# Four pool products in front of the second part of a projection, or two in front and two inside it

## The chip, the cores and the metric

The kernel runs on one core of a Trainium2 chip. The metric is the time of one execution on the device in microseconds; before the change the median of three runs is 1624.82 us (1624.4 to 1625.36). The profiled execution took 1629.18 us, of which the trace spans 1627.4 us. The engines are TensorE (PE in the rows, PEld for its weight loads), VectorE (DVE), ScalarE (ACT), GpSimd (POOL) and SyncE (SP), which issues the weight loads from memory.

## What is computed

Two transformer blocks on 256 rows of width 2048. The change lies in the second block, in what stands between its input projection and its feed-forward part:

```python
h = rms_norm(x, g_mix)
z_pool, z_q, z_kv, z_kr, z_mq = split(h @ w_in)
y_pool = pool_mixer(z_pool, w_pool, pool_scale)   # 4 groups of 128 columns
y_mla = mla_mixer(z_q, z_kv, z_kr, ...)           # 8 heads of 128
y_mem = memory_cross_attention(z_mq, mem, ...)    # 4 heads of 128
x = x + concatenate([y_pool, y_mla, y_mem]) @ w_o
x = x + conv_glu_ffn(rms_norm(x, g_ffn), ...)

# pool_mixer, for group gi with window w:
d = (csum - lagged csum) / count - p              # difference to a running mean
y = einsum('bsgc,gcd->bsgd', d, w_pool) * pool_scale
```

So the row of 2048 values that `w_o` multiplies has sixteen pieces of 128: pieces 0 to 3 are the pool groups, 4 to 11 the heads of the latent attention ("mla"), 12 to 15 the heads of the cross attention.

## The kernel before

All data are kept transposed, 128 features on the partitions and 256 rows along the free axis. A projection is done in blocks: one block is a piece kt of the contraction (128 values) for one tile j of 128 output columns. Operands are split into a high and a low part of reduced width, and a block of the projections spoken of here is three matmuls of 256 columns, L1130 (high weights, high data), L1131 (high, low) and L1132 (low, high). Eight blocks make a "half": the weights of a half lie in a slot of `wh` and `wl`, and ScalarE makes the high part of them (L1480) and VectorE the low part (L1877) of each half, four slots in turn. SyncE loads the raw weights two halves at a time.

The order of all work is made by a planner at build time. It walks through the products, counts estimated costs of each engine, and puts the small steps of the attention heads (six lanes of tasks) between the blocks. What comes out is one list of beats, and every engine runs through its own beats of that list in that order. Nothing on an engine can pass an instruction that waits. The calls of `pool_end` stand outside the planner's costs: they put a beat into the list and take a PSUM bank, no more.

The second output projection (`w_o`) is done in three parts, since the pieces get ready at different times: "oa" contracts over kt 12 to 15, "ob" over kt 4, 5, 6, 7, 0, 1 in this order, "o2" over kt 8 to 11, 2 and 3. Each part goes over all sixteen tiles j, and each tile is then added to `xs` by VectorE (L2311). A tile takes the next of four PSUM banks in rotation (`gemm_bank`), and its first matmul waits until what stood in that bank has been taken out (`bank_clear`).

A pool group ends in `pool_end`: TensorE multiplies the group's 128 x 256 values with its 128 x 128 matrix in full width (L1451, recorded as two passes), VectorE scales the result out of PSUM (L2323), ScalarE writes its high part (L1837), VectorE its low part (L2325). In VectorE's program the scale waits for the product and the low part for ScalarE, before the next group's scale is come to:

```python
e.wait_ge(*after(t, "pe", "mm"))
e.tensor_scalar(y, ps[bank][:, 0:T], v_("pool_scale", g), None, ALU.mult)
e.wait_ge(*after(t, "act", "hi"))
e.tensor_tensor(hB2[:, g, T:2 * T], y, hB2[:, g, 0:T].bitcast(F32), ALU.subtract)
```

Around the change the list reads: the last tiles of "oa"; the value tile "uv" of heads 4 to 7 in banks 3 and 0, which ScalarE copies out (L1755); steps of heads 4, 6 and 7 (scores of head 6, norm of head 4); `pool_end` of groups 0 to 3 in banks 1, 2, 3, 0; weight split 227; "ob" 0 in bank 1, with the maximum of head 6; "ob" 1 to 3 in banks 2, 3, 0, and between their blocks the splits 228 and 229, the scores of head 4 (L1345) after fifteen blocks of "ob", head 4's maximum (L2078 on VectorE), the rest of head 7's norm; after "ob" 3 the turning of head 6's probabilities (L1352), split 230, the first block of "ob" 4, the scores of head 7, the copy of head 6's turned probabilities out of PSUM (L1623 on ScalarE), the next block, and head 6's product of probabilities and values (L1356, L1358). Heads 4 to 7 are pieces 8 to 11, so they have to be ready for "o2". Behind "o2" stands the sum of squares for the next norm: ScalarE squares each tile (L1827), GpSimd adds them up (L2434), and TensorE sums over the partitions (L1393).

Of the kernel before, what the change touches and what calls it, by code (L numbers as in the profile page):

```python
# [17 lines left out]
KT = D // P  # L18
# [178 lines left out]
class Order:  # L197
# [219 lines left out]
    def s_tile(self, tile, buf, order=range(KT), bank=None):  # L417
        if bank is None:
            bank = self.gemm_bank()
            self.take(tile, bank)  # L420
        order = list(order)
        blocks = [(tile, bank, kt, i == 0, i == KT - 1) for i, kt in enumerate(order)]
        self.s_half(blocks[:8], buf)
        self.s_half(blocks[8:], buf)
# [67 lines left out]
def order():  # L492
    o = Order()
# [192 lines left out]
    def up(g, keys):  # L686
        hs = range(4 * g, 4 * g + 4)
        if "un" in keys:
            o.many([("un", h) for h in hs], 0, 2, "L")
        if "uv" in keys:  # L690
            banks = o.gemm_bank(), o.gemm_bank()
            for b in banks:
                o.take(("uv", g), b)
            o.m_half(("uv", g), banks, (0, 1), "L", True, True)
        if "uq" in keys:
            o.many([("uq", h) for h in hs[:2]], 8, 4, "L")
            o.many([("uq", h) for h in hs[2:]], 8, 4, "L")
        if "ur" in keys:
            o.many([("ur", j) for j in (2 * g, 2 * g + 1)], 8, 4, "L")
        o.up_half = o.half  # L700
# [5 lines left out]
    def o2_part(i, first, end):  # L706
        name, kts = O2_PARTS[i]
        blocks = []
        for j in range(first, end):
            b = o.gemm_bank()  # L710
            o.take((name, j), b)
            blocks += [((name, j), b, kt, kt == kts[0], kt == kts[-1]) for kt in kts]
        for u in range(0, len(blocks), 8):
            o.s_half(blocks[u:u + 8], "D")
# [12 lines left out]
    def pool_end(g, bank):  # L727
        o.take(("pf", g), bank)
        o.beat("pf", g, bank)
# [25 lines left out]
    o.until(*[("mem", j) for j in range(4)])  # L755
    o2_part(0, 0, KT)
    up(1, ("uv",))
    for g in range(4):
        pool_end(g, o.gemm_bank())
    o.until(*[("mla", h) for h in range(4)])  # L760
    o2_part(1, 0, KT)
    o.until(*[("mla", h) for h in range(4, 8)])
    o2_part(2, 0, KT)
    o.o2_half = o.half
# [50 lines left out]

def program(nc, table, wts, ada, xN, xT, memN, crow, cst, vec, msk, wpool, dt, out):
    o = order()
    with ExitStack() as ctx:
        at = [nc.sbuf_base + (-nc.sbuf_base) % 32]
# [1769 lines left out]
```

## Time and profile before

| what | value |
|---|---|
| median of three runs | 1624.82 us (1624.4 to 1625.36) |
| the profiled execution | 1629.18 us |
| its span in the trace | 1627.4 us |
| TensorE busy | 1581.8 us (97%) |
| VectorE busy | 1154.2 us (71%) |
| ScalarE busy | 861.7 us (53%) |
| GpSimd busy | 139.6 us (9%) |
| DMA, mean over the span | 203 GB/s |

Shares are of the span. Busy time of TensorE is modelled from pipelined matmuls, so the stretches and the starts of instructions say more of its pace than its busy share. The granted clock is given as a share of full speed; 0.50 is 1.2 GHz and 1.00 is 2.4 GHz. "Idle before" in brackets is the time in which the engine stood still ahead of an instruction, with what released it. Times in the views are counted from the start of the span.

### The profile page before, as it was taken

What the parts mean: (1) busy time and instruction counts of PE and PEld (TensorE: products, weight loads), DVE (VectorE), ACT (ScalarE), POOL (GpSimd) and SP (SyncE); (2) the same over time, 40 slices, a digit from 0 to 9 for tenths busy, and PEclk for the clock granted to TensorE, in tenths of its full rate; (3) what the DMA queues carried; (4) which work ended last, traced back from release to release, by engine and by line L of the source; (5) the groups of instructions that cost most, each with busy time, mean ns of one, the idle gap of its engine ahead of it and who ended that gap; (6) DMA issues with size and microseconds to landing.
All of it is one profiled execution on the core that took longest, in us unless ns stands there. A gap on an engine that the chain in (4) does not pass through costs nothing.

```text
span 1627.4 us, 24289 instructions
## 1 busy us (share of the span) xinstructions
PE 1581.8 (97%) x9650; PEld 1406.2 (86%) x9650; DVE 1154.2 (71%) x1696; ACT 861.7 (53%) x1321; POOL 139.6 (9%) x164
## 2 busy tenths in 40 slices
PE   8899999988999999899899999999999999999999
PEld 6787789988999999887799888888888888888887
DVE  6887867977678876657677777777777777555544
ACT  6755446678655455555556554444444444444442
POOL 0000000311120220034204000000000000000000
PEclk9999999999999999998999999999999999999999
DMA  9999975523556864342244445555545545555552
GB/s 373 357 356 345 361 280 210 204 92 111 194 185 245 316 241 170 132 156 79 78 149 163 173 172 199 184 188 198 199 173 197 198 174 197 207 184 204 183 205 104
DMA packets 47825, 331.02 MB, mean 203 GB/s; under 512 B 5281, under 2 KB 6689, under 8 KB 8417
## 3 DMA queue, kind: packets, MB, share of 16 engines
q1 hardware_dynamic: 45184, 312.20, 52.5%
q0 software_dynamic: 2240, 17.04, 2.7%
q8 instruction: 76, 1.25, 0.3%
q10 hardware_dynamic: 290, 0.25, 0.1%
q14 instruction: 35, 0.29, 0.1%
HBM read 327.37 MB, written 2.10 MB: 202 GB/s over the span
## 4 chain that ended last, share of the span: by engine, by line
PE 73%; DVE 12%; ACT 6%; DMA 4%; issue 3%; POOL 2%; SPq 0%; ACTq 0%; POOLq 0%; DVEq 0%
PE ps L1134 19%; PE ps L1135 10%; PE ps L1130 6%; PE ps L1131 6%; PE ps L1132 6%; PE ps L1188 5%; PE ps L1187 5%; PE ps L1189 5%; DVE wl L1877 4%; DMA raw<-in_wts 3%; ACT wh L1480 2%; DVE raw L1923 2%; PE ps L1177 1%; PE ps L1179 1%; PE ps L1178 1%
## 5 line engine op out<-in xcount | busy, mean ns | idle before, releaser
L1877 DVE TENSOR_TENSOR wl<-raw,wh 128x1024 fp32r<-128x1024 f32 x512 | 624.6, 1233 | 349.0 <-ACT wh L1480 348.6
L1480 ACT ACTIVATE wh<-raw 128x1024 fp32r<-128x1024 f32 x512 | 530.9, 1054 | 369.1 <-PE ps L1189 130.6
L1134 PE MATMUL ps<-hA,wh 128*128 128x512 f32 x1408 | 490.1, 391 | 0.0
L1135 PE MATMUL ps<-hA,wl 128*128 128x256 f32 x1408 | 397.6, 282 | 0.0
L1134 PEld LDWEIGHTS ps<-hA,wh 128*128 128x128 f32 x1408 | 265.1, 188 | 55.6
L1135 PEld LDWEIGHTS ps<-hA,wl 128*128 128x128 f32 x1408 | 266.8, 189 | 0.1
L1130 PE MATMUL ps<-hA,wh 128*128 128x256 f32 x752 | 220.7, 293 | 0.0
L1131 PE MATMUL ps<-hA,wh 128*128 128x256 f32 x752 | 212.5, 283 | 0.0
L1132 PE MATMUL ps<-hA,wl 128*128 128x256 f32 x752 | 212.2, 282 | 0.0
L1130 PE MATMUL ps<-hB,wh 128*128 128x256 f32 x576 | 166.9, 290 | 6.9 <-DVE work L2323 3.4
L1131 PE MATMUL ps<-hB,wh 128*128 128x256 f32 x576 | 163.2, 283 | 0.0
L1132 PE MATMUL ps<-hB,wl 128*128 128x256 f32 x576 | 162.9, 283 | 0.0
L1130 PEld LDWEIGHTS ps<-hA,wh 128*128 128x128 f32 x752 | 143.9, 191 | 2.8 <-issue 2.2
L1131 PEld LDWEIGHTS ps<-hA,wh 128*128 128x128 f32 x752 | 144.0, 192 | 0.8 <-issue 0.2
L1132 PEld LDWEIGHTS ps<-hA,wl 128*128 128x128 f32 x752 | 143.8, 191 | 0.0
L1187 PE MATMUL ps<-wh,hB 128*128 128x512 f32 x352 | 137.0, 389 | 0.0
L1188 PE MATMUL ps<-wl,hB 128*128 128x512 f32 x352 | 136.9, 389 | 0.0
L1189 PE MATMUL ps<-wh,hB 128*128 128x512 f32 x352 | 136.9, 389 | 0.0
L1130 PEld LDWEIGHTS ps<-hB,wh 128*128 128x128 f32 x576 | 110.6, 192 | 12.1 <-issue 9.8
L1131 PEld LDWEIGHTS ps<-hB,wh 128*128 128x128 f32 x576 | 110.7, 192 | 0.3 <-issue 0.2
L1132 PEld LDWEIGHTS ps<-hB,wl 128*128 128x128 f32 x576 | 110.6, 192 | 0.0
L1177 PE MATMUL ps<-wh,hA 128*128 128x512 f32 x256 | 101.0, 395 | 4.7 <-ACT xs L1662 2.7
(303 smaller groups left out, 2067.3 us busy)
## 6 DMA issues: line engine op xcount, KB each, us to landing
raw<-in_wts SPq DMA_DIRECT2D x256, 1024.0 KB, 4.8
raw<-in_ada SPq DMA_DIRECT2D x36, 1024.0 KB, 6.6
side<-in_ada POOLq DMA_DIRECT2D x12, 1024.0 KB, 9.0
work<-in_memN SPq DMA_DIRECT2D x2, 1024.0 KB, 8.9
xs<-in_xN POOLq DMA_DIRECT2D x1, 2048.0 KB, 20.8
xs<-in_xT POOLq DMA_DIRECT2D x2, 1024.0 KB, 7.5
out_rows<-xs SPq DMA_DIRECT2D x8, 256.0 KB, 2.5
wp<-in_dt SPq DMA_DIRECT2D x8, 128.0 KB, 2.3
```

What stands on the lines that cost most here:

```text
L1130: e.matmul(po, w1, hl[:, 0:T], start=first, stop=False)
L1131: e.matmul(po, w1, hl[:, T:2 * T], start=False, stop=False)
L1132: i = e.matmul(po, w2, hl[:, 0:T], start=False, stop=last)
L1134: e.matmul(ps[bank][:, :], w1, hl, start=first, stop=False)
L1135: i = e.matmul(ps[bank][:, T:2 * T], w2, hl[:, 0:T], start=False, stop=last)
L1177: e.matmul(po, hi, w1, start=kt == kts[0], stop=False)
L1187: e.matmul(po, hi, w1, start=first, stop=False)
L1188: e.matmul(po, hi, w2, start=False, stop=False)
L1189: return e.matmul(po, lo, w1, start=False, stop=last)
L1480: e.activation(wh[:, h % WS, :], raw[:, n % RAW, part * HALF:(part + 1) * HALF], ACT.Copy).then_inc(s_hi)
L1877: e.tensor_tensor(wl[:, h % WS, :], src, wh[:, h % WS, :].bitcast(F32), ALU.subtract).then_inc(s_lo)
L1923: e.tensor_tensor_reduce(src, src, cbt, 1.0, 0.0, ALU.mult, ALU.add, c).then_inc(mark(t, "dve", "ttr"))
```

## The change

The calls of `pool_end` for groups 2 and 3 are moved from in front of the part "ob" to behind its fourth tile. The part is called in two pieces for it, tiles 0 to 3 and tiles 4 to 15; four tiles of six blocks are 24 blocks, three whole halves, so halves and weights stay as they are. With the two calls moves all that a pool group issues: its product, its scale, its high and its low part. The banks go on in rotation: "ob" 0 and 1 take banks 3 and 0, "ob" 2 and 3 banks 1 and 2, groups 2 and 3 banks 3 and 0, and "ob" 4 and 5 banks 1 and 2. No instruction is added or taken away.

```diff
     up(1, ("uv",))
-    for g in range(4):
+    for g in range(2):
         pool_end(g, o.gemm_bank())
     o.until(*[("mla", h) for h in range(4)])
-    o2_part(1, 0, KT)
+    o2_part(1, 0, 4)
+    for g in range(2, 4):
+        pool_end(g, o.gemm_bank())
+    o2_part(1, 4, KT)
     o.until(*[("mla", h) for h in range(4, 8)])
     o2_part(2, 0, KT)
```

## Rows read from the trace of the kernel before

**Rows 1.** The head of the page.

```profile
span 1627.4 us, 24289 instructions
```

**Rows 2.** TensorE's waits over the span: total us, times, longest us.

```profile
PE ps L1130 <- DVE work L2323: 3.4, 1, 3.4
...
PE ps L1393 <- POOL work L2434: 2.7, 1, 2.7
...
PE ps L1130 <- issue: 2.4, 1, 2.4
...
PE ps L1378 <- ACT xs L1632: 2.0, 1, 2.0
```

**Rows 3.** The chain that ended last, in order of time, at 857 us.

```profile
856.82 0.13 PE ps L1132
856.99 0.04 issue
857.03 1.07 ACT wh L1480
```

**Rows 4.** Busy us (count) of PE, PEld, DVE, ACT, POOL, then clock, DMA share, GB/s.

```profile
806.60:812.00 5.40, 5.39 (x25) 5.40 (x26) 3.08 (x8) 2.52 (x5) 0.00 (x0) 0.50 0.01 3
...
831.80:887.00 55.20, 55.20 (x465) 54.38 (x464) 37.65 (x65) 31.51 (x57) 12.85 (x13) 1.00 0.47 172
```

**Rows 5.** Instructions in order of time, 799 to 809 us: start us, us, engine, line.

```profile
799.53 1.08 ACT L1755 ACTIVATE work<-ps 128x512 f32<-128x512 f32 x2 [1.67 <-PE ps L1155]
...
801.25 1.99 PE L1451 MATMUL ps<-work,wp 128*128 128x256 f32 x8
...
806.00 0.47 DVE L2323 TENSOR_SCALAR work<-ps,vs 128x256 f32<-128x256 f32 x1
806.50 0.42 ACT L1837 ACTIVATE hB<-work 128x256 fp32r<-128x256 f32 x1 [4.70 <-DVE work L2323]
...
806.61 0.55 PE L1130 MATMUL ps<-hB,wh 128*128 128x256 f32 x1 [3.37 <-DVE work L2323]
...
806.95 0.43 DVE L2325 TENSOR_TENSOR hB<-work,hB 128x256 fp32r<-128x256 f32 x1 [0.48 <-ACT hB L1837]
...
807.29 0.48 DVE L2323 TENSOR_SCALAR work<-ps,vs 128x256 f32<-128x256 f32 x1
...
808.25 0.43 DVE L2325 TENSOR_TENSOR hB<-work,hB 128x256 fp32r<-128x256 f32 x1 [0.48 <-ACT hB L1837]
```

**Rows 6.** TensorE in order of time: scores, turning and values product of heads 4 and 6.

```profile
814.46 0.82 PE L1345 MATMUL ps<-late 128*128 128x128 f32 x4
...
821.44 0.49 PE L1352 MATMUL ps<-cs,work 128*128 128x128 f32 x3
...
824.18 0.59 PE L1356 MATMUL ps<-work 128*128 128x256 f32 x2
```

**Rows 7.** VectorE in order of time, 816 to 827 us.

```profile
816.17 0.29 DVE L2078 CUSTOM_DVE_ANT_0 work<-ps,cs 128x128 f32<-128x128 f32 x1 [0.58 <-PE ps L1345]
...
822.15 0.41 DVE L2311 TENSOR_TENSOR xs<-xs,ps 128x256 f32<-128x256 f32 x1
...
823.08 0.41 DVE L2311 TENSOR_TENSOR xs<-xs,ps 128x256 f32<-128x256 f32 x1
823.40 1.21 DVE L1877 TENSOR_TENSOR wl<-raw,wh 128x1024 fp32r<-128x1024 f32 x1
...
826.43 0.42 DVE L2311 TENSOR_TENSOR xs<-xs,ps 128x256 f32<-128x256 f32 x1 [0.99 <-PE ps L1132]
```

**Rows 8.** ScalarE in order of time: group 3's high part, two weight splits, head 6's copy.

```profile
810.41 0.42 ACT L1837 ACTIVATE hB<-work 128x256 fp32r<-128x256 f32 x1 [0.89 <-DVE work L2323]
810.73 1.04 ACT L1480 ACTIVATE wh<-raw 128x1024 fp32r<-128x1024 f32 x1
...
821.69 1.06 ACT L1480 ACTIVATE wh<-raw 128x1024 fp32r<-128x1024 f32 x1 [0.17 <-PE ps L1132]
822.66 0.47 ACT L1623 ACTIVATE work<-ps 128x384 f32<-128x384 f32 x1
```

**Rows 9.** The stretches behind two other waits of TensorE, columns as in Rows 4.

```profile
382.00:385.40 3.40, 3.40 (x12) 2.89 (x13) 1.33 (x3) 2.31 (x8) 1.35 (x3) 0.51 0.18 41
...
690.30:693.70 3.40, 3.29 (x24) 3.03 (x25) 1.99 (x2) 1.15 (x3) 2.64 (x4) 1.00 0.16 19
```

## The prediction

> **What bounds the kernel now.** I read the page first, then who TensorE waited for over the whole span, then the stretch around the four pool products in three views: busy time and clock by stretch, instructions in order of time on each engine, and the chain that ended last. The span is 1627.4 us [rows 1] and TensorE is the bound nearly everywhere. Its waits are few [rows 2], and one lies exactly where the change is made: 3.4 us in front of a matmul of L1130, released by the VectorE scaling L2323 of a pool product. After it the engine stands in no wait until the second output projection is over; there it waits 2.7 us for the chain of squares on GpSimd (L1393), and that chain is itself started by TensorE, at 857.03 [rows 3]: it moves along with TensorE. After 897 us the list of TensorE's waits is empty. So whatever delay or gain stands on TensorE at about 830 us reaches the end of the kernel whole, and the question is what TensorE does between 801 and 830 us.
>
> In that stretch [rows 4, 5]: the four products run from 801.25 for 1.99 us (eight passes, two to a product). TensorE is then idle to 806.61. Nothing about the products is late: VectorE is still working through the norm of MLA head 4, and comes to the scaling of pool group 0 only at 806.00. The first "ob" tile stands in the bank of group 0's product and may not start before that scaling. The idle time also costs clock: the granted clock is 0.50 from 806.60 to 812.00, that is the 1.2 GHz level, with 25 matmuls in 5.40 us (0.216 us each, 0.65 us for a block of three), where a later full-clock stretch has 465 in 55.20 us (0.119 each, 0.36 a block).
>
> **What the change does, part by part.**
>
> *The products leave a hole and go where there is none.* Two products are half of 1.99 us, 1.0 us of TensorE. Before, all four lay in front of an idle stretch, so two of them cost nothing. Afterwards they stand behind "ob" 3, where TensorE has work queued and no wait. That is +1.0 us on the path.
>
> *Four blocks move into the hole.* The banks rotate, so "ob" 0 and 1 now follow the value tile "uv" in its banks 3 and 0, which ScalarE's copies (L1755, begun at 799.53) emptied before the products [rows 5]. "ob" 0 can start at 801.25 + 1.0 = 802.25 and does its blocks for kt 4 to 7, 4 x 0.36 = 1.4 us, until 803.7. Its fifth block needs the low part of pool group 0, L2325, which starts at 806.95 and takes 0.43: 807.38; with the 0.14 us that lay between the end of the scaling (806.47) and the matmul (806.61) it starts at about 807.5. The sixth needs group 1's low part, 808.25 + 0.43 = 808.68, so 808.8. These times are VectorE's and do not move, since nothing of the change stands ahead of them. Ten more blocks follow before the scores of head 4 (L1345, 814.46 before [rows 6]). If the clock comes back at 812.0 as before, they are 3.2/0.65 = 4.9 slow ones and 5.1 x 0.36 = 1.8 us more: 813.8, or 0.65 us early. If it comes back 5.4 us after the restart at 807.5, it is 814.25, 0.2 us early. I take 0.4 us early, call this shift s = -0.4, and keep as bounds that the clock does not fall at all (808.8 + 10 x 0.36 = 812.4, s = -2.1) and that all ten are slow (815.3, s = +0.85).
>
> *VectorE's and ScalarE's part of the two groups moves too.* Each group is scale on VectorE (L2323), high part on ScalarE (L1837), low part on VectorE (L2325), each waiting for the one before; the groups follow each other at 1.30 us (806.00 to 807.29) [rows 5]. Before, groups 2 and 3 had these 2.6 us while TensorE was in the first "ob" tiles and the queues behind held only weight splits and head 6's maximum, for which TensorE did not wait. In the changed order they stand behind the addition of "ob" 3 on VectorE and ahead of weight split 230 (L1480, L1877) and of head 6's copy of its turned probabilities (L1623) on ScalarE. TensorE waits for that copy: it is the operand of head 6's product with its values, L1356 at 824.18 [rows 6]. VectorE is busy without a hole from the maximum of head 4 (816.17), which TensorE's scores release, to the addition of "ob" 3 (L2311, 823.08) and the split at 823.40 [rows 7]; all of it moves by s. Then group 2's scaling starts at 823.40 + s, group 3's at 824.70 + s, and group 3's high part on ScalarE 0.50 us later (806.00 to 806.50) at 825.20 + s. Split 230 follows 0.32 us behind it (810.41 to 810.73), the copy 0.97 us behind the split (821.69 to 822.66) and takes 0.47 [rows 8]: 825.20 + 0.32 + 0.97 + 0.47 = 826.96 + s. Head 6's product can start at about 827.0 + s. TensorE reaches it at 824.18 + s + 1.0 = 825.2 + s. So a new wait of 1.8 us follows, and the product stands 2.8 + s = +2.4 us later than before.
>
> *Banks.* "ob" 4 now follows "ob" 2 in its bank instead of "ob" 0. Its addition starts at 822.15 + s and takes 0.41 [rows 7]: 822.56 + s. TensorE comes there behind head 6's turning (L1352 from 821.44) and the products, not before 822.44 + s. The wait is at most some 0.3 us, and it would only be taken off the 1.8 us behind it. The two products need banks of "ob" 0 and 1, long added. "ob" 6 and 7 need groups 2 and 3 scaled (825.1 + s), and come after the new wait. The low parts of groups 2 and 3 are read first by the third part, "o2".
>
> *What moves earlier.* Splits 227 and 228 come up to 2.6 us sooner on both engines, since the two groups no longer stand ahead of them. TensorE did not wait for them, so this is worth nothing. No DMA is issued by what moved; the loads wait for splits, and the one behind split 230 or 231 is delayed some 3 us with several halves of about 3 us of split weights in hand.
>
> *Behind it.* From "ob" 4's addition on, VectorE waited for TensorE before (0.99 us idle ahead of 826.43), so both move together. Sum: -0.4 (clock and four blocks) + 1.0 (products) + 1.8 (new wait) = **+2.4 us**. Against the profiled execution that is 1629.18 + 2.4 = 1631.6 us; that execution lies 4.4 us above the median of the runs, and I carry the difference over: 1624.82 + 2.4 = **1627.2 us**. Its own range by the bounds of s is +0.7 to +3.65.
>
> **The rivals.** *The clock falls in the new wait as well (slower).* The rows show both outcomes for waits of this size: behind the 2.0 us wait of L1378 the clock was 0.51 for 3.4 us, behind a wait of 2.4 us at 690.3 it stayed at 1.00 [rows 2, 9]. If it falls, 3.4 us at half clock cost 1.7 us: 2.4 + 1.7 = +4.1, 1628.9 us, and with the upper bound of s 1630.2. [...] The Trainium skill, TensorE: Matmul & The Clock Gate, section A second HAM failure mode: psum-queue depth-cycling, says that short idles between groups of matmuls can make the clock swing between its levels; by it this rival would be the likelier one. The row at 690.3 speaks against it as a rule. Chance 0.30.
>
> *No new wait.* VectorE and ScalarE were released earlier around 811 us; if they turn that into a lead, or the planner's other work leaves ScalarE free sooner, the copy is in time and only the products' own time stays: 1.0 - 0.4 = +0.6, 1625.4 us. Against it: VectorE waits for TensorE's scores at 816.17 (0.58 us idle), so a lead from before is lost there. Chance 0.13.
>
> *The clock holds over the first hole.* The four blocks fill part of it. With s = -2.1 and no new wait it would be -1.1, 1623.7 us; even then it is no gain that can be told. Against it: what is left of the hole is 3.8 us, longer than the 3.37 us that brought the clock down. Chance 0.05. That the edit would not do what it says can be left aside: the second part contracts over kt 4 to 7, 0 and 1, so groups 2 and 3 are free to come later.
>
> **How the numbers follow.** Forecast 0.52, clock falls again 0.30, no new wait 0.13, clock holds 0.05. Predicted 1627.2. The range 1625.0 to 1630.2 takes in the forecast's bounds almost whole, the first rival and the second. A measurement of this kernel tells about 0.2%, 3.25 us, from no change. The forecast lies inside that but for its upper end, the second and third rivals inside, the first one mostly beyond: same 0.64, slower 0.33, faster 0.03.
>
> **What would show it.** In the profile after: L1451 in two groups of four passes, the second near 822 us; the 3.4 us wait before L1130 released by L2323 gone, and in its place one of about 3.8 us released by L2325 and one of some 0.6 us; a new wait of about 1.8 us before L1356, released by ScalarE's L1623; L1345 of head 4 between 813.8 and 815.3. I am wrong if L1356 starts without a wait, if the granted clock is not at its low level behind the first hole, or if TensorE's lateness at 830 us is not found again at the end.

## The result, and the profile after

The changed kernel takes 1629.26 us in the median of 20 runs, the kernel before 1625.36 us in as many; the ratio is 1.0021 with a 95% interval of 1.0012 to 1.0030, that is +3.4 us (+2.0 to +4.9). The forecast was +2.4 us, and 1627.2 us from a base of 1624.82. The difference of +2.4 lies inside the measured interval; the time is 2.1 us (0.13%) above the forecast, and 0.5 us of that is the base.

The profiled execution doesn't show this at first sight. It took 1628.31 us with a span of 1626.5 us, less than the 1627.4 us of [rows 1]. The reason lies ahead of the change: the products start at 797.92 us here and at 801.25 before [rows 5], 3.33 us sooner, after work that is the same in both. From the start of the products on, the comparison is clean, and it is made in two pieces. From there to the sum over partitions behind "o2" it is 92.63 us before (801.25 to 893.88) and 95.10 us after (797.92 to 893.02), and from that sum to the end 733.52 and 733.48 us. So the loss is +2.5 us in this pair, and all of it lies between the products and the end of the second output projection.

The waits of TensorE in the changed kernel, 795 to 870 us (the lines of the file stand three further down, L1130 is now L1133; total us, times, longest):

```profile
PE ps L1133 <- DVE hB L2328: 4.3, 2, 3.6
PE ps L1359 <- ACT work L1626: 1.8, 1, 1.8
```

In place of the one wait of [rows 2] for the scaling there are two for the low parts of groups 0 and 1, and a new one for ScalarE's copy. TensorE in order of time:

```profile
797.92 1.13 PE L1454 MATMUL ps<-work,wp 128*128 128x256 f32 x4
798.70 0.47 PE L1133 MATMUL ps<-hB,wh 128*128 128x256 f32 x1
...
804.10 0.39 PE L1133 MATMUL ps<-hB,wh 128*128 128x256 f32 x1 [3.63 <-DVE hB L2328]
...
805.41 0.58 PE L1133 MATMUL ps<-hB,wh 128*128 128x256 f32 x1 [0.69 <-DVE hB L2328]
...
810.57 0.82 PE L1348 MATMUL ps<-late 128*128 128x128 f32 x4
...
817.54 0.49 PE L1355 MATMUL ps<-cs,work 128*128 128x128 f32 x3
817.87 1.03 PE L1454 MATMUL ps<-work,wp 128*128 128x256 f32 x4
818.81 0.36 PE L1133 MATMUL ps<-hB,wh 128*128 128x256 f32 x1
...
823.21 0.67 PE L1359 MATMUL ps<-work 128*128 128x256 f32 x2 [1.76 <-ACT work L1626]
```

Two products (four passes), four blocks, the hole, the fifth block, a short wait, ten blocks, the scores of head 4; then behind the turning of head 6 the other two products, and a wait of 1.76 us in front of head 6's values product. What it waits for is seen on ScalarE, in order of time:

```profile
820.02 0.42 ACT L1840 ACTIVATE hB<-work 128x256 fp32r<-128x256 f32 x1 [2.39 <-DVE work L2326]
821.32 0.42 ACT L1840 ACTIVATE hB<-work 128x256 fp32r<-128x256 f32 x1 [0.89 <-DVE work L2326]
821.65 1.04 ACT L1483 ACTIVATE wh<-raw 128x1024 fp32r<-128x1024 f32 x1
822.59 0.47 ACT L1626 ACTIVATE work<-ps 128x384 f32<-128x384 f32 x1
```

ScalarE is idle for 2.39 us, with the weight split and the copy ready behind it, since the instruction at its head waits for VectorE. Before, the same copy followed the split at 822.66 without any of this [rows 8]. And VectorE comes to the scaling only behind the addition of "ob" 3:

```profile
819.18 0.41 DVE L2314 TENSOR_TENSOR xs<-xs,ps 128x256 f32<-128x256 f32 x1
819.51 0.47 DVE L2326 TENSOR_SCALAR work<-ps,vs 128x256 f32<-128x256 f32 x1
```

### The profile page after: what moved, and what is told of

Read it like the earlier page. It is cut to its first block, busy times and chain, and to the rows that moved or that the text cites. A ratio compares the mean times of both kernels' runs of the same rounds, so it can differ in the third digit from the quotient of the medians.

```text
span 1626.5 us, 24289 instructions
## 1 busy us (share of the span) xinstructions
PE 1579.8 (97%) x9650; PEld 1405.4 (86%) x9650; DVE 1154.0 (71%) x1696; ACT 861.8 (53%) x1321; POOL 139.7 (9%) x164
## 4 chain that ended last, share of the span: by engine, by line
PE 77%; DVE 12%; ACT 5%; DMA 3%; issue 2%; POOL 1%; SPq 0%; ACTq 0%; DVEq 0%; POOLq 0%
PE ps L1137 20%; PE ps L1138 10%; PE ps L1133 7%; PE ps L1134 6%; PE ps L1135 6%; PE ps L1191 5%; PE ps L1190 5%; PE ps L1192 5%; DVE wl L1880 4%; DVE raw L1926 2%; PE ps L1180 2%; PE ps L1182 2%; PE ps L1181 2%; ACT wh L1483 2%; DMA xs<-in_xN 1%
## 5 line engine op out<-in xcount | busy, mean ns | idle before, releaser
L1133 PE MATMUL ps<-hA,wh 128*128 128x256 f32 x752 | 220.6, 293 | 0.0
L1133 PE MATMUL ps<-hB,wh 128*128 128x256 f32 x576 | 166.7, 289 | 7.8 <-DVE hB L2328 4.3
L1133 PEld LDWEIGHTS ps<-hA,wh 128*128 128x128 f32 x752 | 143.9, 191 | 2.8 <-issue 2.2
L1133 PEld LDWEIGHTS ps<-hB,wh 128*128 128x128 f32 x576 | 110.2, 191 | 13.4 <-issue 6.4
```

Of the source, the lines that this page charges most:

```text
L1133: e.matmul(po, w1, hl[:, 0:T], start=first, stop=False)
```

## Experiments

The kernels of the experiments ran 12 times each, e_after_shift6 6 times, against 29 to 35 executions of the kernel before. In the table, "to values" is the time from TensorE's first pool product to head 6's values product, "to sum" that from the same start to the sum over partitions behind "o2"; "wait" is the wait in front of the values product alone. "Ratio" is that of the execution times, the other columns are read from one profile each. For the kernels where groups 0 and 1 come early, the start would be another, so the last column counts from the last matmul of the value tile "uv" (799.10 us before) to that sum.

| kernel | to values | wait | to sum | uv to sum | ratio to before (interval) |
|---|---|---|---|---|---|
| before | 22.93 | none | 92.63 | 94.78 | 1 |
| changed | 25.29 | 1.76 | 95.10 | 97.25 | 1.0021 (1.0012 to 1.0030) |
| e_parked | 25.29 | 2.77 | 96.50 | 98.62 | 1.0027 (1.0015 to 1.0039) |
| e_behind_max | 24.33 | none | 94.11 | 96.23 | 1.0008 (0.9994 to 1.0022) |
| e_group3 | 23.44 | 1.03 | 93.24 | 95.36 | 1.0010 (0.9997 to 1.0022) |
| e_tile12 | 22.34 | none | 92.92 | 95.08 | 1.0006 (0.9995 to 1.0016) |
| e_before_shift3 | 22.96 | none | 92.67 | 94.79 | 1.0001 (0.9986 to 1.0016) |
| e_after_shift3 | 25.26 | 1.75 | 95.05 | 97.22 | 1.0028 (1.0013 to 1.0043) |
| e_before_shift6 | 22.96 | none | 92.66 | 94.82 | 1.0016 (1.0005 to 1.0027) |
| e_after_shift6 | 25.25 | 1.74 | 96.46 | 98.61 | 1.0043 (1.0026 to 1.0060) |
| e_early01_late23 | | none | | 91.30 | 0.9971 (0.9957 to 0.9986) |
| e_early_all | | none | | 93.01 | 1.0005 (0.9991 to 1.0019) |
| e_early01 | | none | | 96.80 | 1.0015 (1.0001 to 1.0030) |

### Is it the products, or what stands in front of the copy?

Products first, the rest of the two groups late. The beat of `pool_end` is taken apart into TensorE's part ("pf") and the other engines' ("pe"). The edit in short:

```diff
-    o2_part(1, 0, 4)
     for g in range(2, 4):
-        pool_end(g, o.gemm_bank())
+        o.take(("pf", g), 3)          # two halves of bank 3
+        o.beat("pf", g, 3)
+    o.ring = (0, 1, 2)                # banks of the four tiles
+    o2_part(1, 0, 4)
+    for g in range(2, 4):
+        o.beat("pe", g, 3)
+    o.ring = (0, 1, 2, 3)
     o2_part(1, 4, KT)
```

> The changed kernel, but the products of pool groups 2 and 3 on TensorE stay in front of the part 'ob', as before; they wait in the two halves of one bank, and only their scaling, high part and low part (VectorE, ScalarE) stand behind the fourth tile. The first four tiles use the other three banks. Theory (the new wait is set by what stands ahead of head 6's copy in ScalarE's and VectorE's queues): the two products, 1.0 us, are taken off TensorE's path, but the copy comes no earlier, so the wait in front of head 6's values product grows from 1.76 us to about 2.75 us; from the start of the products to that values product it stays at 25.3 us (22.9 before the change), and the time stays at that of the changed kernel, +2.4 to +3.4 us against before. Rival (the products' own time on TensorE is what costs): the wait stays 1.76 us or less, 24.3 us, and 1.0 us less than the changed kernel.

TensorE of this kernel, in order of time:

```profile
797.80 1.99 PE L1467 MATMUL ps<-work,wp 128*128 128x256 f32 x8
...
803.99 0.39 PE L1146 MATMUL ps<-hB,wh 128*128 128x256 f32 x1 [2.79 <-DVE hB L2341]
...
823.09 1.19 PE L1372 MATMUL ps<-work 128*128 128x256 f32 x2 [2.77 <-ACT work L1639]
```

Its clock behind the later wait (us of the stretch, busy of PE, PEld, DVE, ACT, POOL, then clock, DMA share, GB/s):

```profile
822.70:826.00 3.30, 2.91 (x11) 2.76 (x12) 1.92 (x7) 1.78 (x4) 0.00 (x0) 0.50 0.00 0
```

The hole is shorter by 0.8 us and the later wait longer by 1.0 us, and the 25.29 us stand to the hundredth. With the wait there, the products' own time costs nothing; taking it away gains nothing. The queue of VectorE and ScalarE is what sets the values product. That the sum behind "o2" comes 1.4 us later than in the changed kernel (96.50 for 95.10) comes with the low clock of that row.

The other way round: TensorE's order untouched, the two groups on VectorE and ScalarE some beats later ("pf" and "pe" are taken apart as above, not shown again).

```diff
+    ends = [b for b in o.beats if b[0] == "pe" and b[1] >= 2]
+    o.beats = [b for b in o.beats if b not in ends]
+    at = o.beats.index(("t", ("mla", 7), "max")) + 1
+    o.beats[at:at] = ends
```

> The changed kernel with TensorE's order untouched; only the scaling, high part and low part of groups 2 and 3 are moved some beats further back, from in front of split 230 to behind head 7's maximum, so that split 230 and head 6's copy go first. Theory: the wait of 1.76 us in front of head 6's values product is gone; what stays is 1.0 us of products less 0.56 us gained by the four blocks and the clock, so products' start to values product is about 23.4 us, and the time is +0.4 to +0.6 us against before, with no other wait up to the end of the projection. Rival (product time, or the clock): the loss stays at +2.4 us or more. A third outcome would be that VectorE, which had 1.0 us of idle time in front of the addition of tile 4, passes some 1.6 us on to head 5's scores.

ScalarE in order of time, and TensorE's waits between 790 and 880 us:

```profile
819.71 1.06 ACT L1488 ACTIVATE wh<-raw 128x1024 fp32r<-128x1024 f32 x1 [0.20 <-PE ps L1140]
820.68 0.47 ACT L1631 ACTIVATE work<-ps 128x384 f32<-128x384 f32 x1
...
824.09 0.42 ACT L1845 ACTIVATE hB<-work 128x256 fp32r<-128x256 f32 x1 [1.56 <-DVE work L2331]
```

```profile
PE ps L1138 <- DVE hB L2333: 3.9, 2, 3.6
```

The split and the copy go ahead of the high part now. The wait is gone, and nothing else waits from the first hole to the end of the projection. The measured loss is 1.3 us with an interval that holds none and the expected 0.5 us; the trace gives +1.5 us (94.11 against 92.63). The 0.9 us over the expectation go with the clock. Its granted level over two stretches behind the first hole:

```profile
805.00:811.60 6.60, 6.27 (x27) 5.97 (x28) 4.67 (x11) 4.20 (x8) 0.00 (x0) 0.50 0.35 124
811.70:813.00 1.30, 1.30 (x11) 1.17 (x10) 0.00 (x0) 0.14 (x2) 0.00 (x0) 0.93 0.30 126
```

(Columns as above.) TensorE runs at 1.2 GHz for 6.6 us here, for 5.4 us before [rows 4], and for 3.3 us in the changed kernel (805.40 to 808.70). So head 4's scores come 13.59 us behind the products' start (798.86 to 812.45) instead of 13.21: a shift s of +0.4 in place of -0.56, and 0.4 + 0.94 is 1.3 of the 1.5 us.

Half the change, only group 3 behind tile 4:

```diff
-    for g in range(2):
+    for g in range(3):
         pool_end(g, o.gemm_bank())
...
-    for g in range(2, 4):
+    for g in range(3, 4):
         pool_end(g, o.gemm_bank())
```

> Only group 3 stands behind the fourth tile; groups 0 to 2 are in front of the part as before. Half of the change. Theory: one group less in front of the copy, 1.30 us, and one product less on TensorE, 0.5 us: the wait in front of head 6's values product is 1.76 - 1.30 + 0.5 = about 1.0 us, products' start to values product about 24.0 us, +1.1 us against before. If the cost were the product on TensorE alone, there would be no wait and -0.56 + 0.5 = about 0 us. If the clock over the first idle stretch made the loss, it would be as large as in the changed kernel.

The wait is 1.03 us, as the queue has it; products alone would have none. The time to the values product is 23.4 instead of 24.0 us, and again the rest is in the low stretch:

```profile
808.90:812.20 3.30, 2.91 (x12) 2.62 (x13) 1.81 (x5) 1.78 (x3) 0.00 (x0) 0.51 0.00 0
```

It is as long as in the changed kernel, but starts with the fifth block instead of the sixth, so that part of it falls on the short wait (0.39 us): 12 matmuls are in it, where the changed kernel has 15. Head 4's scores come 12.10 us behind the products' start (802.69 to 814.79), 0.55 us sooner than there.

Both groups behind the twelfth tile, where all heads are done:

```diff
-    o2_part(1, 0, 4)
+    o2_part(1, 0, 12)
     for g in range(2, 4):
         pool_end(g, o.gemm_bank())
-    o2_part(1, 4, KT)
+    o2_part(1, 12, KT)
```

> The changed kernel with groups 2 and 3 behind the twelfth tile of 'ob' instead of the fourth; groups 0 and 1 as they were. All heads are done there, so nothing that TensorE waits for stands behind the two groups. Theory: the first idle stretch is as in the changed kernel (3.6 and 0.7 us), there is no other wait, and only the products' 1.0 us less 0.56 us stays: +0.4 to +0.6 us against before, products' start to the sum of squares behind 'o2' about 93.1 us (92.6 before, 95.1 in the changed kernel). If it stays above 94.5 us, the place in the queues was not the cause.

TensorE's waits between 790 and 880 us:

```profile
PE ps L1133 <- DVE hB L2328: 4.3, 2, 3.6
```

There is no wait but the two in the first hole (3.65 and 0.69 us), and 92.92 us against 92.63, +0.3 us; the ratio of 1.0006 (+1.0 us, -0.8 to +2.6) doesn't contradict it. The same instructions at another place in the same list cost 2.2 us less by the traces (92.92 for 95.10).

### Does the clock fall in the new wait?

Kernels before and after with three and six repeats of the first sum over partitions, which move all that follows:

```diff
+                    for _ in range(3 * (t[1] == 0)):      # or 6
+                        e.matmul(ps[bank][:, 0:T], ones[:], rm3, start=True, stop=True)
                     e.matmul(ps[bank][:, 0:T], ones[:], rm3, start=True, stop=True).then_inc(mark(t, "pe", "ss"))
```

> The kernel before with three repeats of the first small sum over partitions (the one whose result all of the second block's input projection waits for), which starts everything behind it about 1.3 us later. It moves the stretch against the times at which the clock is switched. Theory: the idle stretch in front of 'ob' is 3.4 us as before, and from the products' start to head 6's values product it takes 22.9 us if the clock falls for as long as before (5.4 us), and 1.7 us less or more where the low stretch lies otherwise. It is the base for the changed kernel with the same shift.

> The changed kernel with the same shift of about 1.3 us. Theory: the wait in front of head 6's values product is 1.8 us again, and against the kernel before with this shift the loss is 2.4 us plus or minus what the low clock does to either. Rival (the clock makes the rest of the measured +3.4 us): in some placement the clock falls in the new wait, too, and the loss is about 4 us there.

> The kernel before with six repeats, about 2.6 us later. The same expectation as for three repeats, at another place against the switching of the clock: between 21.2 and 24.6 us from the products' start to head 6's values product.

> The changed kernel with the same shift of about 2.6 us. Theory: the same wait of 1.8 us, and a loss of 2.4 us against its base but for the clock. Rival: a second low stretch behind the new wait, seen as a granted clock of 0.50 for 3.4 us after it, and a loss of about 4 us.

The kernel before is the same in all three profiles, 92.63, 92.67 and 92.66 us. The changed one is 95.10, 95.05 and 96.46. In the last one the low clock comes with the new wait:

```profile
825.40:827.10 1.70, 0.02 (x1) 0.00 (x0) 0.85 (x2) 1.70 (x4) 0.00 (x0) 0.88 0.56 236
827.20:829.80 2.60, 2.60 (x10) 2.42 (x11) 1.49 (x7) 1.35 (x3) 0.00 (x0) 0.50 0.02 6
829.80:832.00 2.20, 2.20 (x20) 2.20 (x19) 1.07 (x3) 0.35 (x1) 0.00 (x0) 0.93 0.00 0
```

Ten matmuls in 2.60 us where the changed kernel's own profile has 27 in 3.40 us at 1.00:

```profile
823.20:826.60 3.40, 3.39 (x27) 3.35 (x28) 2.56 (x9) 1.65 (x4) 0.00 (x0) 1.00 0.02 5
```

The price is 96.46 - 95.10 = 1.4 us. e_parked, with its longer wait of 2.77 us, shows it too (96.50). So of three profiles with the wait of 1.74 to 1.76 us one has the low clock behind it, and with e_parked it is two of four. The repeats did not place the stretch as meant, since executions differ by as much at that point on their own (the products start between 797.8 and 804.5 us in these profiles); they served as further samples. In the runs each changed kernel stands 0.0027 above its own base, 4.4 us; the intervals overlap that of the main comparison, and they neither show nor exclude a mean price of the clock.

### A version that is faster than both

Groups 0 and 1 right behind the value tile, ahead of the norm of head 4; groups 2 and 3 behind the twelfth tile:

```diff
     # on top of e_tile12
+    first = [b for b in o.beats if b[0] == "pf" and b[1] < 2]
+    o.beats = [b for b in o.beats if b not in first]
+    at = o.beats.index(("ev", ("uv", 1))) + 1
+    o.beats[at:at] = first
```

> A candidate. Groups 0 and 1 are put right behind the value tile 'uv', ahead of the steps of heads 4, 6 and 7 that stood between (so VectorE scales them before the norm of head 4), and groups 2 and 3 behind tile 12 of 'ob', when all heads are done. Theory: the idle stretch of 3.4 us in front of 'ob' goes, and with it its low clock (5.4 us at half, 2.7 us); head 4's norm comes 2.6 us later, and TensorE waits for it in front of head 4's scores, some 1 us; the two products cost 1.0 us where they now stand. In sum 3.4 + 2.7 - 1.0 - 1.0 = about 4 us faster than before, less what VectorE, busy nearly all the time from 811 to 826 us, can't follow: between -4 and -1 us. Rival: VectorE is the bound of the whole stretch, the idle time only moves, and the time is that of before within 1 us.

It is 4.7 us faster than before (2.3 to 7.0), where -4 to -1 was expected. Its waits in this part, in order of time:

```profile
794.55 0.67 PE L1458 MATMUL ps<-work,wp 128*128 128x256 f32 x2 [0.54 <-DVE xs L2318]
...
803.19 0.89 PE L1352 MATMUL ps<-late 128*128 128x128 f32 x4 [0.97 <-POOL work L2430]
...
811.75 0.89 PE L1352 MATMUL ps<-late 128*128 128x128 f32 x4 [0.67 <-POOL work L2430]
```

The hole of 3.37 us has become 2.2 us in three pieces, none of which brought the clock down. From "uv" to the sum it is 91.30 instead of 94.78 us, -3.5 us. In this profile the clock held behind the sum, too, worth 1.6 us (731.92 to the end, 733.52 before). Both together are 5.1 us in this pair of profiles.

Two kernels show which half does it. Groups 0 and 1 early, 2 and 3 left in front of "ob":

```diff
     # on top of the kernel before
+    first = [b for b in o.beats if b[0] == "pf" and b[1] < 2]
+    o.beats = [b for b in o.beats if b not in first]
+    at = o.beats.index(("ev", ("uv", 1))) + 1
+    o.beats[at:at] = first
```

> The kernel before with groups 0 and 1 right behind the value tile, ahead of the norm of head 4, and groups 2 and 3 where they were. It takes the early half of the candidate alone. Theory: the idle stretch in front of 'ob' goes, the two late products cost nothing extra on TensorE, but VectorE has the 2.6 us of groups 2 and 3 ahead of split 227 and head 6's maximum in the busy stretch, so some wait comes back in front of head 4's scores or head 6's turning: 2 to 4 us faster than before, about as fast as the candidate (-4.7 us) or 1 to 2 us behind it.

The expectation failed: 2.4 us slower than before (0.2 to 4.9), not faster; +2.0 us in the trace. Its two larger waits:

```profile
810.22 0.38 PE L1134 MATMUL ps<-hB,wh 128*128 128x256 f32 x1 [1.52 <-DVE work L2327]
...
821.66 1.45 PE L1349 MATMUL ps<-late 128*128 128x128 f32 x4 [2.38 <-POOL work L2427]
```

TensorE now starts "ob" without a hole, but the third tile stands in group 2's bank and waits for its scaling, and head 7's scores wait for a norm that VectorE reaches late. I had counted the queue and not the bank. The granted clock was 0.50 from 821.9 to 828.6, behind the second of these waits, which the trace shows and my estimate had not.

All four early, the same edit without the condition `b[1] < 2`:

> The kernel before with all four groups right behind the value tile, ahead of head 4's norm. Theory: that norm comes 5.2 us later, and TensorE, which is no longer idle in front of 'ob', waits for it some 3 us in front of head 4's scores: the idle stretch has moved and the kernel is 0 to 3 us faster than before. Rival (only the place of groups 0 and 1 matters): as fast as with groups 0 and 1 early.

TensorE's waits between 790 and 880 us:

```profile
PE ps L1349 <- POOL work L2427: 3.4, 2, 2.7
PE ps L1455 <- DVE xs L2315: 0.6, 1, 0.6
```

The 2.7 us in front of head 4's scores were expected as some 3 us. The trace gives -1.8 us (93.01 against 94.78), the runs can't tell it from nothing. So of the placements tried only the two halves together gave a gain that the runs show: groups 0 and 1 early, and groups 2 and 3 behind the heads, out of the stretch in which VectorE is busy. Either half alone didn't, nor did all four early, where the wait comes back in front of head 4's scores.

## Why the prediction was right

Each step of the sum, by the changed kernel's own trace:

- *Four blocks in the hole, s.* They ran from 798.70, and the hole became 3.63 and 0.69 us, where 3.8 and 0.6 were said. Head 4's scores came 12.65 us behind the products' start (797.92 to 810.57) instead of 13.21: s = -0.56, for -0.4. The clock was low for one stretch only, with all the work from 805.4 to 808.7 at 0.50. That it fell at all, which the third rival doubted, all profiles with this hole show.
- *The two products.* 817.87 to 818.81, 0.94 us for 1.0.
- *The bank of "ob" 4.* No wait.
- *The new wait.* 1.76 us, for 1.8, released by the instruction named. The two groups' rhythm on VectorE is 1.30 us again (819.51 to 820.81), the high part of group 3 to the split 0.33 us, the split to the copy 0.94 us.
- *Sum.* 22.93 to 25.29 us, +2.36 us, for +2.4. Of -0.56 + 0.94 + 1.76 = 2.14 it is 0.2 us more: 0.1 us around the products (turning to products 0.33 us, turning to the next block 0.24 before), the rest because a wait is counted from the modelled end of the matmul ahead of it. That the sum lists the products and the wait as two terms is only a way of counting: the time of the copy, 827.0 + s, holds no product, and e_parked shows that +2.4 us stay when the products are taken out.
- *Nothing takes it back.* +2.5 us at the sum behind "o2", the rest 733.48 us for 733.52.

What was too small is the place given to the first rival. The forecast holds for an execution in which the clock stays up behind the new wait, and one of three profiles of this order is not such; it is 1.4 us longer, for the 1.7 us that I had said. One in three makes +2.9 us in the mean, two in four with e_parked about +3.1, and I had forecast the likeliest case rather than the mean. Whether this is what separates +2.4 from +3.4 us isn't shown: all of these values, the forecast too, lie in the measured +2.0 to +4.9, so that the missing 1.0 us may as well be noise.

The chance of 0.30 rested on two waits of [rows 2, 9], one with a fall and one without. That was a choice among rows. The same trace has six waits of 2.0 to 2.7 us on TensorE, ending at 46.73, 150.21, 333.82, 381.97, 690.30 and 893.88 us, and the one at 690.30 is the only one without a fall. Behind the four not shown so far (columns as above):

```profile
47.60:51.00 3.40, 3.40 (x10) 2.63 (x9) 3.33 (x7) 0.98 (x2) 0.53 (x1) 0.50 0.78 313
150.00:153.40 3.40, 3.19 (x8) 2.54 (x9) 3.22 (x5) 2.44 (x5) 0.00 (x0) 0.50 0.82 301
334.30:337.70 3.40, 3.40 (x15) 3.03 (x15) 1.22 (x8) 3.23 (x12) 0.00 (x0) 0.50 0.05 16
...
894.10:897.50 3.40, 3.40 (x11) 2.84 (x11) 2.71 (x4) 1.55 (x4) 0.00 (x0) 0.50 0.19 60
```

So the rows on hand spoke for a larger chance than 0.30, and the row at 690.3 was the exception. The section of the Trainium skill named in the prediction (TensorE: Matmul & The Clock Gate, A second HAM failure mode: psum-queue depth-cycling) speaks of idles that come back between groups of matmuls again and again, and gives no odds for a single wait; at this wait the traces have a fall in one of three, or two of four with e_parked. How often the clock falls in unprofiled runs, and what decides it, stays open: the granted clock by stretch is known only for the profiles.

The second rival, no new wait, is excluded by all four kernels that have the queue of the changed one. That the lead from splits 227 and 228 is lost at head 4's scores was right: VectorE waited 1.83 us for them, 0.58 before [rows 7].

## What to carry to other kernels

An operation that goes to and fro between two engines that each work off one list in order should be counted by what stands behind it on both, not by its own work: here two groups with 2.6 us of to and fro cost TensorE 1.8 us in one place and nothing eight tiles later, while the 0.9 us of TensorE's own work that moved with them was free as long as the wait was there. An idle stretch of the bounding engine hides work: the two products cost nothing in it, and 0.9 us behind it where no wait took them up (e_behind_max, e_tile12). To shorten the stretch, ask what it waits for and move that ahead, as the faster version does. And where a new wait arises, its price has two values, with the clock and without; to judge the odds, count every wait of that size in the trace, not one of each kind.

## What the runs showed of the hardware

A wait of 1.74 us with dense work on both sides had TensorE's clock at 1.2 GHz behind it in one execution (e_after_shift6), and one of 1.75 us had not in another (e_after_shift3). Nor is it this place alone: the wait of 1.4 us near 478 us, in code that no edit touches, has a low stretch within 1.8 us of its end in 8 of the 12 profiles that show it, and the wait of 2.0 us near 380 us has one in all 13. Behind the longer one of 2.7 us at 805.6 us in e_early_all there is none. Two executions of kernels that are the same up to that point reach it 3 us apart (797.92 and 801.25 us), and twenty runs of one kernel spread over 7 us (1623.51 to 1630.70 us), while the piece from the products to the sum repeats within 0.05 us in the three profiles of the kernel before, and in the changed one, too, but for the case with the low clock (95.10, 95.05 and 96.46). For an edit of this size the piece is the better measure of each case; the ratio of 12 or 20 runs, with an interval 3 to 6 us wide, tells neither case from the other nor how often they occur.
